# The low halves of a mixer's weights move from GpSimd to VectorE

## The chip, the cores and the metric

One NeuronCore of a Trainium2 chip runs one program. The metric is the device time of one execution in microseconds (us), taken as the median of three runs. The engines are named as the profile names them: PE is TensorE, DVE is VectorE, ACT is ScalarE, POOL is GpSimd, SP is SyncE. Each engine carries out its own instructions in the order in which the program lists them, and engines wait for one another on semaphores.

## The reference, cut to what matters

Two layers of a trunk are applied to 128 context tokens and 128 latent tokens. Each layer is a token mixer and then a channel mixer (a dense one in layer 0, eight experts in layer 1). The change touches the token mixer alone:

```python
u = h @ P['w_in'][l]                       # 1024 -> 9216: queries, keys, values, gates
...                                        # retention, neighbourhood attention, gated recurrence
proj = jnp.einsum('nbtw,nwd->btnd', br, P['w_br'][l])
gates = jax.nn.sigmoid(mg.reshape(B, T, N_BRANCH, D_MODEL))
out = jnp.sum(gates * proj, axis=2) @ P['w_o'][l]
```

So a layer's mixer has three large products: with `w_in`, with `w_br` (three branches, each then multiplied by a gate and added up) and with `w_o`.

## The kernel before, in words

**Split products.** A 32-bit product is made from three products of operands that were split into a high and a low half: `product` (line 949) issues high times low, low times high and high times high (lines 951 to 953), each 512 columns wide. So every weight block exists three times: as loaded (`ring`), its high half (`m_hi`, written by ACT in `mix_split`, line 700), and its low half (`ring_lo`, loaded value minus high half, a subtraction of 128x2048 elements by DVE at line 1630 or by POOL at line 551).

**Slabs and units.** The mixer of a layer reads 23 slabs in a fixed order: panels 0 to 13 of `w_in`, branch 0 of `w_br`, panels 14 and 15, branch 1, panels 16 and 17, branch 2, and two halves of `w_o`. Each slab is two units of 2048 columns, numbered m = 0 to 45; unit m belongs to slab m // 2. A panel of `w_in` is slab c = j up to panel 13; panel 14 is slab 15, panel 15 is slab 16, panel 16 is slab 18, panel 17 is slab 19. There are three buffers for high halves, so ACT may make the high half of unit m only when PE has finished unit m - 3 (`mix_used`).

**The order on each engine** is written out by hand:

- PE runs panel j, then small products of the branches (`pieces`), and after panels 13, 15 and 17 the projection of a branch (`project`), followed for the first two by one step of the recurrence (`level`, line 1013). `panel(l, j)` for j of 14 or more begins with a wait on `pr_read`: the first half of branch 0's projection must have been read from its PSUM bank before panel 14 can write there, the second half before panel 15, and the same for branch 1 with panels 16 and 17.
- ACT makes the high half of one unit before it reads a finished panel and of one after it; at a branch it makes two more.
- DVE calls `ahead(l, kind, i)` once for each slab c. It makes the low halves of units 2c + 3 and 2c + 4. Between these calls stand the steps of the branches: `level_read` (line 1607) and `products` (lines 1592 to 1603, eight multiplications of 128x512) for the recurrence, `heads_turned` (line 1613), and `gated` (lines 1647 and 1650), which multiplies the projection of a branch by its gate, half by half, and by that counts up `pr_read`. Directly ahead of `gated(l, 0)` stands `ahead(l, "br", 0)` with units 31 and 32, and directly ahead of `gated(l, 1)` stands `ahead(l, "br", 1)` with units 37 and 38.
- POOL holds a list `POOL_UNITS`: the first units of slabs 12 to 19, that is m = 24, 26, 28, 30, 32, 34, 36 and 38. For these DVE's `mix_split` returns at once, and POOL makes the low half as soon as the high half is there. POOL's low halves are counted on a semaphore of their own (`mix_lo_pool`); PE's `unit` asks `mix_lo_made` which semaphore and which count to wait for.

Of the kernel before, what the change touches and what calls it, by code (L numbers as in the profile page):

```python
# [20 lines left out]
F32 = mybir.dt.float32  # L21
# [3 lines left out]
ALU = mybir.AluOpType  # L25
# [20 lines left out]
UNIT = 2048  # L46
# [38 lines left out]
MIX_SLABS = [[key for key in layer_slabs(l) if key[0] in ("win", "br", "wo")] for l in range(L)]  # L85
MIX_UNITS = 2 * len(MIX_SLABS[0])
STEP = {key[0:1] + key[2:]: c for c, key in enumerate(MIX_SLABS[0])}


POOL_UNITS = [2 * c + 4 for c in range(STEP["win", 10], STEP["win", 15] + 2)]  # L90


def ring_plan():

    uses, before, at, plan = [0] * SLOTS, [None] * SLOTS, 0, {}
    for l in range(L):
        todo = layer_slabs(l)
        if l == 0:
            todo += [("ffn", 0, i) for i in range(NFS)]
        for key in todo:  # L100
            s = at % SLOTS
            at += 1
            if key[0] != "skip":
                plan[key] = (s, uses[s], before[s])
                uses[s] += key[0] != "ffn"
                before[s] = key
    assert at % SLOTS == 0
    return plan, before


def program(nc, x, c_t, b_mod_t, norm_t, lb_t, decay, hgn, rpb, cache_kt, cache_v, s_ret, s_hg, router, consts, levels,
            w_mod, w_in, w_br, w_o, w_ff, y, new_k, new_v, new_ret, new_hg):
    plan, before0 = ring_plan()
    dense_loads = [len(range(s, NFS, SLOTS)) for s in range(SLOTS)]

    with ExitStack() as ctx:
# [3 lines left out]
        def sem(name):  # L120
            return ctx.enter_context(nc.semaphore(name))

        def shared(whole, parts):

            with ExitStack() as first:
# [4 lines left out]
        ring, ring_lo = [r[0][0] for r in rings], [r[1][0] for r in rings]  # L130
# [16 lines left out]
        m_hi = [r[:, 2 * UNIT:3 * UNIT] for r in ring_lo]  # L147
        rv_hi = rv_hi.rearrange("p (g c) -> p g c", g=2)
        rg_hg = rg_hg.rearrange("p (g c) -> p g c", g=2)
        nv = nv.rearrange("p (g c) -> p g c", g=2)  # L150
        (gate,), (pick_r, pickT_r, _) = shared([("gate", 2 * D)], [("pick", 2 * 2 * P), ("pickT", 2 * 2 * P), ("gate_rest", D)])
        gates = gate.rearrange("p (g c) -> p g c", g=2)
        q_dec = gate[:, 0:2 * W].rearrange("p (d h t) -> p d h t", d=2, h=H)
        decays = gate[:, 2 * W:3 * W].rearrange("p (h t) -> p h t", h=H)
        bias = gate[:, 3 * W:4 * W].rearrange("p (h t) -> p h t", h=H)
        (u,), (_, act_hi, act_lo, hr_hi, hr_lo, eo_hi, eo_lo) = shared(
            [("u", 11 * D)], [("u_head", 2 * D), ("act_hi", W), ("act_lo", W), ("hr_hi", 2 * D), ("hr_lo", 2 * D),
                              ("eo_hi", 2 * D), ("eo_lo", 2 * D)])
# [76 lines left out]
        def con_(name):  # L235
            return con[:, CONST_AT[name]:CONST_AT[name] + CONST_W[name]]
# [83 lines left out]
        brt_read = sem("brt_read")  # L320
        mix_hi = sem("mix_hi_ready")
        mix_lo = sem("mix_lo_ready")
        mix_lo_pool = sem("mix_lo_pool_ready")
        mix_half = sem("mix_half_used")
        mt_hi = sem("merged_hi_ready")
        lev_ready = sem("lev_ready")
# [64 lines left out]
        def mix_unit(l, m):  # L391

            return MIX_SLABS[l][m // 2], m % 2, (MIX_UNITS * l + m) % SLOTS, MIX_UNITS * l + m

        def mix_lo_made(l, m):

            if m in POOL_UNITS:
                return mix_lo_pool, len(POOL_UNITS) * l + POOL_UNITS.index(m) + 1
            return mix_lo, (MIX_UNITS - len(POOL_UNITS)) * l + m + 1 - sum(v < m for v in POOL_UNITS)

        def mix_used(l, m):

            key, half, _, count = mix_unit(l, m)
            return released(key) if half else (mix_half, count // 2 + 1)
# [93 lines left out]
        @block.gpsimd  # L498
        def _(pool):
            pool.dma_start(cond, c_t).then_inc(s_cond, 16)  # L500
            for dst, src in ((con, consts), (bm, b_mod_t), (ng, norm_t), (lbr, lb_t), (dec, decay),
                             (rout_w, router), (level_mask, levels)):
                pool.dma_start(dst, src).then_inc(s_const, 16)
            pool.dma_start(x_sb, x).then_inc(s_x, 16)

            def power(out, in_, done, n):
                pool.tensor_tensor(out, in_, con_("half")[:, 0:1].broadcast_to([P, n]), ALU.pow).then_inc(done, 1)

            for l in range(L):
                if l:  # L510

                    pool.wait_ge(pr_read, 6 * l)
                pool.dma_start(bias, rpb[l]).then_inc(s_bias, 16)
                if l:

                    pool.wait_ge(pv_done, l)
                    pool.wait_ge(ho_done, l)
                pool.dma_start(ckT, cache_kt[l]).then_inc(s_cache, 16)
                pool.dma_start(cv, cache_v[l]).then_inc(s_cache, 16)
                pool.dma_start(state0, s_ret[l]).then_inc(s_sret, 16)  # L520
                if l:
                    pool.wait_ge(br_ready, 3 * l)
                pool.dma_start(hgn_sb, hgn[l]).then_inc(s_hgn, 16)
                if l == 0:
                    pool.wait_ge(s_const, 16 * 7)
                pool.wait_ge(ms_ready, 4 * l + 1)
                power(rs, ms, rs_ready, 2)

                pool.wait_ge(kd_ready, 1)
                pool.wait_ge(win_read, NWIN * l + 2)  # L530
                for d in range(2):
                    for h in range(H):
                        last = pool.tensor_scalar(kdec[:, d, h * HD:(h + 1) * HD], stage[:, 1, 0, h * HD:(h + 1) * HD],
                                                  kd[:, l, d, h:h + 1], None, ALU.mult)
                last.then_inc(kdec_ready, 1)
                pool.wait_ge(ve_ready, l + 1)
                power(hrs, hms, rsr_ready, 8)
                pool.wait_ge(win_read, NWIN * l + 6)
                pool.dma_start(new_k[l], stage[:, 1, 0, :]).then_inc(s_kout, 16)
                pool.wait_ge(win_read, NWIN * l + 7)  # L540
                pool.dma_start(new_v[l], nv[:, 0, :]).then_inc(s_vout, 16)
                pool.wait_ge(rst_read, l + 1)
                pool.dma_start(new_ret[l], state_out).then_inc(s_srout, 16)
                pool.wait_ge(ro_done, l + 1)
                pool.dma_start(state0, s_hg[l]).then_inc(s_shg, 16)
                for m in POOL_UNITS:
                    key, half, b, count = mix_unit(l, m)
                    s = plan[key][0]
                    part = slice(half * UNIT, (half + 1) * UNIT)
                    pool.wait_ge(mix_hi, count + 1)  # L550
                    pool.tensor_tensor(ring_lo[s][:, part], ring[s][:, part], m_hi[b].bitcast(F32), ALU.subtract)\
                        .then_inc(mix_lo_pool, 1)
                pool.wait_ge(hms_ready, l + 1)
                power(hrs, hms, hrs_ready, 8)
                pool.wait_ge(hst_read, l + 1)
                pool.dma_start(new_hg[l], state_out).then_inc(s_shout, 16)
                for n in (1, 2, 3):
                    pool.wait_ge(ms_ready, 4 * l + n + 1)
                    power(rs, ms, rs_ready, 2)
            pool.wait_ge(x_new, 2 * L)  # L560
            pool.dma_start(y, x_sb).then_inc(s_yout, 16)
# [350 lines left out]
        def _(pe):  # L912
# [42 lines left out]
            def unit(l, step, half, blocks):  # L955

                pe.wait_ge(*mix_lo_made(l, 2 * step + half))
                key, half, b, count = mix_unit(l, 2 * step + half)
                pe.wait_ge(mix_hi, count + 1)
                lo = ring_lo[plan[key][0]][:, half * UNIT:(half + 1) * UNIT]  # L960
                return [v.rearrange("p (k c) -> p k c", k=blocks) for v in (m_hi[b], lo)]
# [443 lines left out]
        def _(dve):  # L1405
# [215 lines left out]

            def mix_split(l, m):

                if m in POOL_UNITS:
                    return
                key, half, b, count = mix_unit(l, m)
                s = plan[key][0]
                dve.wait_ge(mix_hi, count + 1)
                part = slice(half * UNIT, (half + 1) * UNIT)
                V.tensor_tensor(ring_lo[s][:, part], ring[s][:, part], m_hi[b].bitcast(F32), ALU.subtract).then_inc(mix_lo, 1)  # L1630

            def ahead(l, kind, i):

                for m in (2 * STEP[kind, i] + 3, 2 * STEP[kind, i] + 4):
                    mix_split(l, m)
# [184 lines left out]
            for l in range(L):  # L1820
# [3 lines left out]
                if l:  # L1824
                    mix_split(l, 0)
# [9 lines left out]
                if l == 0:  # L1835
                    mix_split(0, 0)
                    own(read_mod(1), mod_read, 1)
                    modulation(0, 2, 6, mod_raw[:, 8 * MOD_FIRST:2 * NMOD], mod_rest, 1)
# [191 lines left out]
```

## Time and profile before

| | |
|---|---|
| median of three runs (lowest, highest) | 1937.44 us (1936.02, 1938.24) |
| time of the profiled execution | 1936.62 us |
| its span in the profile | 1934.8 us |
| mean granted clock of PE | 0.963 of full speed |
| busy: PE, DVE, ACT, POOL | 93%, 65%, 51%, 7% of the span |

The span is what the profiler sees from the first to the last instruction; the execution's own time is 1.8 us longer. Stages in time: modulation until about 170 us, mixer of layer 0 from there to about 499 us, the dense channel mixer until about 740 us, mixer of layer 1 to about 1067 us, and the experts until the end. The units in question are used between about 320 and 440 us and between about 888 and 1007 us. In the timeline each line gives the start, the duration, engine, line and operation, and in brackets the idle time before it on its engine and what ended it. In layer 1 the same instructions stand 567 us later with nearly the same durations, so most rows below are of layer 0.

### The profile page before, as it was taken

Reading aid. Unit: us, or ns where it says so; the run is one execution under the profiler, and the core shown is the slowest. Engines: PE = TensorE matmul, PEld = TensorE weight load, DVE = VectorE, ACT = ScalarE, POOL = GpSimd, SP = SyncE. Lnnn points to the kernel's source line nnn. Section 1 sums busy time; section 2 is a strip of 40 time slices with the busy share of each in tenths; the row PEclk is TensorE's granted clock in tenths of the full one; section 3 lists DMA queues with packets and bytes.
Section 4 is the critical chain, followed back from the end, with each engine's and each line's share of the span. In section 5 each row is a group of like instructions: output and inputs, shape, how many; then the busy total and the mean of one; then the engine's idle time right before and its main releaser. Section 6 shows DMA issues by size and latency. Waiting matters only on the chain.

```text
span 1934.8 us, 20304 instructions
## 1 busy us (share of the span) xinstructions
PE 1809.0 (93%) x8206; PEld 1414.5 (73%) x8206; DVE 1250.1 (65%) x1053; ACT 988.6 (51%) x966; POOL 126.4 (7%) x78
## 2 busy tenths in 40 slices
PE   8999999997699986999998599999999999999995
PEld 1224888886578865888876578888888888888884
DVE  1102567984354525658884378888888888888883
ACT  2101435333444326345332367777777777777772
POOL 1000201320000000102320000000000000000000
PEclk9999999998899997999998699999999999999998
DMA  9887454341544432454332369989898999898990
GB/s 396 297 305 265 177 200 174 134 172 55 201 169 186 162 138 83 160 207 172 132 131 98 152 239 352 365 334 366 339 358 341 359 345 362 337 366 340 363 372 26
DMA packets 55822, 470.60 MB, mean 243 GB/s; under 512 B 6352, under 2 KB 6400, under 8 KB 8496
## 3 DMA queue, kind: packets, MB, share of 16 engines
q1 hardware_dynamic: 52848, 458.25, 62.2%
q0 software_dynamic: 2880, 11.02, 1.4%
q8 instruction: 68, 1.11, 0.2%
q14 instruction: 26, 0.21, 0.0%
HBM read 465.05 MB, written 4.19 MB: 243 GB/s over the span
## 4 chain that ended last, share of the span: by engine, by line
PE 91%; DVE 3%; ACT 3%; issue 2%; DMA 0%; POOL 0%; POOLq 0%; ACTq 0%; DVEq 0%
PE ps L951 25%; PE ps L952 24%; PE ps L953 24%; PE ps L926 9%; PE ps L1127 2%; PE ps L1013 1%; PE ps L1079 1%; PE ps L1161 1%; PE ps L993 1%; PE ps L945 1%; ACT ring_lo L700 0%; DMA ring<-in_w_mod 0%; ACT wide L627 0%; PE ps L1384 0%; DVE x_sb L1685 0%
## 5 line engine op out<-in xcount | busy, mean ns | idle before, releaser
L1691 DVE TENSOR_TENSOR ring_lo<-ring,w_hi 128x2048 fp32r<-128x2048 f32 x297 | 680.1, 2292 | 178.9 <-ACT w_hi L711 178.2
L951 PE MATMUL ps<-ring_lo,h_both 128*128 128x512 f32 x1520 | 609.0, 401 | 23.7 <-issue 16.3
L711 ACT ACTIVATE w_hi<-ring 128x2048 fp32r<-128x2048 f32 x297 | 567.9, 1915 | 102.7 <-PE ps L953 93.6
L1630 DVE TENSOR_TENSOR ring_lo<-ring,ring_lo 128x2048 fp32r<-128x2048 f32 x76 | 182.6, 2405 | 265.6 <-ACT ring_lo L700 265.0
L951 PEld LDWEIGHTS ps<-ring_lo,h_both 128*128 128x128 f32 x1520 | 288.2, 190 | 82.6 <-issue 24.3
L952 PE MATMUL ps<-w_hi,h_both 128*128 128x512 f32 x880 | 345.6, 393 | 0.0
L953 PE MATMUL ps<-w_hi,h_both 128*128 128x512 f32 x880 | 345.6, 393 | 0.0
L700 ACT ACTIVATE ring_lo<-ring 128x2048 fp32r<-128x2048 f32 x92 | 176.2, 1917 | 323.3 <-PE ps L953 210.7
L952 PE MATMUL ps<-ring_lo,h_both 128*128 128x512 f32 x640 | 251.5, 393 | 0.0
L953 PE MATMUL ps<-ring_lo,h_both 128*128 128x512 f32 x640 | 251.4, 393 | 0.0
L953 PEld LDWEIGHTS ps<-w_hi,h_both 128*128 128x128 f32 x880 | 166.6, 189 | 35.5
L952 PEld LDWEIGHTS ps<-w_hi,h_both 128*128 128x128 f32 x880 | 167.1, 190 | 32.2
L951 PE MATMUL ps<-ring_lo,act_hi 128*128 128x512 f32 x440 | 177.6, 404 | 9.4 <-DVE ring_lo L1691 9.4
L926 PE MATMUL ps<-ring,cond_pad 128*36 128x512 f32 (+1 forms) x384 | 167.7, 599 | 9.4 <-DMA ring<-in_w_mod 9.4
L953 PE MATMUL ps<-w_hi,act_hi 128*128 128x512 f32 x440 | 173.6, 395 | 0.0
L952 PE MATMUL ps<-w_hi,act_lo 128*128 128x512 f32 x440 | 173.4, 394 | 0.0
L953 PEld LDWEIGHTS ps<-ring_lo,h_both 128*128 128x128 f32 x640 | 121.6, 190 | 25.9
L952 PEld LDWEIGHTS ps<-ring_lo,h_both 128*128 128x128 f32 x640 | 121.8, 190 | 24.2
L926 PEld LDWEIGHTS ps<-ring,cond_pad 128*36 128x36 f32 (+1 forms) x384 | 41.6, 109 | 133.7 <-issue 133.7
L951 PEld LDWEIGHTS ps<-ring_lo,act_hi 128*128 128x128 f32 x440 | 83.9, 191 | 25.1 <-DVE ring_lo L1691 9.9
L953 PEld LDWEIGHTS ps<-w_hi,act_hi 128*128 128x128 f32 x440 | 83.6, 190 | 17.8
L952 PEld LDWEIGHTS ps<-w_hi,act_lo 128*128 128x128 f32 x440 | 83.9, 191 | 15.1
(269 smaller groups left out, 1524.8 us busy)
## 6 DMA issues: line engine op xcount, KB each, us to landing
ring<-in_w_ff SPq DMA_DIRECT2D x297, 1024.0 KB, 7.2
ring<-in_w_in SPq DMA_DIRECT2D x36, 2048.0 KB, 7.8
ring<-in_w_mod SPq DMA_DIRECT2D x24, 2048.0 KB, 7.8
ring<-in_w_br SPq DMA_DIRECT2D x6, 2048.0 KB, 7.8
ring<-in_w_o SPq DMA_DIRECT2D x4, 2048.0 KB, 7.7
out<-state_out POOLq DMA_DIRECT2D x4, 512.0 KB, 4.5
x_sb<-in_x POOLq DMA_DIRECT2D x1, 1024.0 KB, 23.7
state<-in_s_ret POOLq DMA_DIRECT2D x2, 512.0 KB, 20.8
```

Source lines behind the costliest of these rows:

```text
L700: A(m_hi[b], ring[s][:, half * UNIT:(half + 1) * UNIT], ACT.Copy).then_inc(mix_hi, 1)
L711: A(w_hi[p], ring[slab_slot(n)][:, p * UNIT:(p + 1) * UNIT], ACT.Copy).then_inc(hi_ready[p], 1)
L926: ins = mm(ps[0:height, part, :], cond_pad[:, k, at:at + height], w[:, k, :], start=(i == 0 and k == 0), stop=(n == slabs[-1] and k == KD ...
L945: ins = nc.tensor.transpose(ps[:, 4 + 2 * g + k // 4, (k % 4) * P:(k % 4 + 1) * P], xn[:, g, k * P:(k + 1) * P], ident)
L951: mm(out, a_hi, b_lo, start=start, stop=False, skip_group_check=True)
L952: mm(out, a_lo, b_hi, start=False, stop=False, skip_group_check=True)
L953: return mm(out, a_hi, b_hi, start=False, stop=stop, skip_group_check=True)
L993: ins = nc.tensor.transpose(ps[:, 6 + g, h * P:(h + 1) * P], src[:, h * HD:(h + 1) * HD], ident)
L1013: ins = mm(ps[:, 6 + u // 4, (u % 4) * P:(u % 4 + 1) * P], k_lev[:, u * P:(u + 1) * P], q[:, u * P:(u + 1) * P], start=True, stop=True)
L1127: ins = mm(out[:, v * P:(v + 1) * P], rows[:, g, k * P:(k + 1) * P], pick[:, b, g, :], start=(g == 0), stop=(g == 1))
L1630: V.tensor_tensor(ring_lo[s][:, part], ring[s][:, part], m_hi[b].bitcast(F32), ALU.subtract).then_inc(mix_lo, 1)
L1691: V.tensor_tensor(ring_lo[slot][:, part], ring[slot][:, part], w_hi[p].bitcast(F32), ALU.subtract)\
```

## The change

The list `POOL_UNITS`, its semaphore and POOL's loop are removed. DVE's `mix_split` no longer skips those units, so `ahead` now makes both of its units on DVE, in program order. PE waits on one semaphore, counted in unit order.

```diff
-POOL_UNITS = [2 * c + 4 for c in range(STEP["win", 10], STEP["win", 15] + 2)]
...
-        mix_lo_pool = sem("mix_lo_pool_ready")
...
         def mix_lo_made(l, m):
 
-            if m in POOL_UNITS:
-                return mix_lo_pool, len(POOL_UNITS) * l + POOL_UNITS.index(m) + 1
-            return mix_lo, (MIX_UNITS - len(POOL_UNITS)) * l + m + 1 - sum(v < m for v in POOL_UNITS)
+            return mix_lo, MIX_UNITS * l + m + 1
...
                 pool.wait_ge(ro_done, l + 1)
                 pool.dma_start(state0, s_hg[l]).then_inc(s_shg, 16)
-                for m in POOL_UNITS:
-                    key, half, b, count = mix_unit(l, m)
-                    s = plan[key][0]
-                    part = slice(half * UNIT, (half + 1) * UNIT)
-                    pool.wait_ge(mix_hi, count + 1)
-                    pool.tensor_tensor(ring_lo[s][:, part], ring[s][:, part], m_hi[b].bitcast(F32), ALU.subtract)\
-                        .then_inc(mix_lo_pool, 1)
                 pool.wait_ge(hms_ready, l + 1)
                 power(hrs, hms, hrs_ready, 8)
...
             def mix_split(l, m):
 
-                if m in POOL_UNITS:
-                    return
                 key, half, b, count = mix_unit(l, m)
                 s = plan[key][0]
                 dve.wait_ge(mix_hi, count + 1)
```

## Rows read from the trace of the kernel before

**Rows 1.** The page: busy time of engines, and the chain's shares by engine.
```profile
PE 1809.0 (93%) x8206; PEld 1414.5 (73%) x8206; DVE 1250.1 (65%) x1053; ACT 988.6 (51%) x966; POOL 126.4 (7%) x78
...
PE 91%; DVE 3%; ACT 3%; issue 2%; DMA 0%; POOL 0%; POOLq 0%; ACTq 0%; DVEq 0%
```

**Rows 2.** Timeline of PE: start, duration, instruction, idle time before it.
```profile
371.15 1.95 PE L1013 MATMUL ps<-u 128*128 128x128 f32 x16
374.72 0.47 PE L951 MATMUL ps<-ring_lo,h_both 128*128 128x512 f32 x1 [1.63 <-issue]
...
415.50 0.47 PE L951 MATMUL ps<-ring_lo,h_both 128*128 128x512 f32 x1 [1.59 <-issue]
...
470.64 2.48 PE L1040 MATMUL ps<-con,wide 128*128 128x128 f32 x16 [3.87 <-DVE wide L1650]
...
942.19 0.47 PE L951 MATMUL ps<-ring_lo,h_both 128*128 128x512 f32 x1 [1.63 <-issue]
...
1038.17 3.36 PE L1040 MATMUL ps<-con,wide 128*128 128x128 f32 x16 [3.87 <-DVE wide L1650]
```

**Rows 3.** Timeline of DVE, layer 0, around products and gates.
```profile
342.71 0.70 DVE L1592 TENSOR_TENSOR u<-u 128x512 f32<-128x512 f32 x1
...
347.79 2.29 DVE L1630 TENSOR_TENSOR ring_lo<-ring,ring_lo 128x2048 fp32r<-128x2048 f32 x1
...
371.19 2.29 DVE L1630 TENSOR_TENSOR ring_lo<-ring,ring_lo 128x2048 fp32r<-128x2048 f32 x1
373.40 2.48 DVE L1647 TENSOR_TENSOR wide<-ps,gate 128x1024 f32<-128x1024 f32 x2
375.91 1.38 DVE L1607 COPY_PREDICATED u<-level_mask,ps 128x1024 f32<-128x1024 int32 x1
...
411.97 2.29 DVE L1630 TENSOR_TENSOR ring_lo<-ring,ring_lo 128x2048 fp32r<-128x2048 f32 x1
414.18 1.22 DVE L1647 TENSOR_TENSOR br<-ps,gate 128x1024 f32<-128x1024 f32 x1
```

**Rows 4.** Timeline of ACT, layer 0: high halves of units 28, 30, 32, 36, 38.
```profile
346.08 1.92 ACT L700 ACTIVATE ring_lo<-ring 128x2048 fp32r<-128x2048 f32 x1
...
359.64 1.92 ACT L700 ACTIVATE ring_lo<-ring 128x2048 fp32r<-128x2048 f32 x1
...
371.40 1.92 ACT L700 ACTIVATE ring_lo<-ring 128x2048 fp32r<-128x2048 f32 x1 [3.52 <-PE ps L953]
...
400.45 1.92 ACT L700 ACTIVATE ring_lo<-ring 128x2048 fp32r<-128x2048 f32 x1
...
412.22 1.91 ACT L700 ACTIVATE ring_lo<-ring 128x2048 fp32r<-128x2048 f32 x1 [3.24 <-PE ps L953]
```

**Rows 5.** Groups of POOL's instructions: count, busy us and mean ns, idle before.
```profile
L551 POOL TENSOR_TENSOR ring_lo<-ring,ring_lo 128x2048 fp32r<-128x2048 f32 x16 | 77.5, 4841 | 218.2 <-ACT ring_lo L700 218.2
```

**Rows 6.** Groups of DVE's instructions between 300 and 437 us.
```profile
L1630 DVE TENSOR_TENSOR ring_lo<-ring,ring_lo 128x2048 fp32r<-128x2048 f32 x13 | 34.2, 2627 | 7.6 <-ACT ring_lo L700 7.3
L1592 DVE TENSOR_TENSOR u<-u 128x512 f32<-128x512 f32 x7 | 16.3, 2335 | 0.0
...
L1571 DVE TENSOR_SCALAR u<-u,olb,lb 128x256 f32<-128x256 f32 x8 | 6.2, 842 | 2.3 <-ACT u L863 2.3
L1650 DVE TENSOR_TENSOR wide<-wide,br 128x1024 f32<-128x1024 f32 x2 | 5.7, 2832 | 0.1
...
L1593 DVE TENSOR_TENSOR u<-u 128x512 f32<-128x512 f32 x7 | 4.8, 684 | 0.0
```

**Rows 7.** Stretches: length, busy PE, PEld, DVE, ACT, POOL, granted clock, DMA.
```profile
374.70:378.70 4.00, 3.98 (x18) 3.29 (x19) 3.96 (x4) 0.00 (x0) 3.31 (x1) 1.00 0.79 340
...
475.40:478.80 3.40, 3.26 (x8) 2.62 (x9) 2.33 (x2) 1.05 (x1) 0.00 (x0) 0.51 0.00 0
...
1038.50:1041.90 3.40, 3.03 (x15) 2.63 (x13) 0.98 (x1) 1.36 (x2) 0.00 (x0) 0.51 0.95 407
...
710.20:714.30 4.10, 4.10 (x10) 3.23 (x11) 0.00 (x0) 0.00 (x0) 0.00 (x0) 0.50 0.35 146
```

## The prediction

> **What bounds the kernel now.** I first read the busy times on the page and the chain of waits: PE is busy 93% of the span and makes 91% of the chain, POOL is busy 7% [rows 1]. So an edit on DVE or POOL moves the time only where PE ends up waiting for it. I then looked for PE's idle stretches in the stage that the change touches. The timeline of PE shows just two per layer worth naming, in the same places: before panel 14, 1.63 us ahead of 374.72, and before panel 16, 1.59 us ahead of 415.50; layer 1 repeats the first at 942.19 and the second likewise, so four in all [rows 2]. The releaser is given as "issue", which tells nothing, so I looked at what the program waits for there: panel 14 needs the first half of `gated(l, 0)`. On DVE's timeline two of line 1647 start at 373.40 and take 2.48 us; the first ends at about 374.62, and PE starts 0.1 us later. The other place fits as well: 414.18 plus 1.22 is 415.40, and PE starts at 415.50 [rows 2, 3]. So DVE's arrival at `gated` sets these two starts, and what DVE has to do just ahead of it is what counts.
>
> **What the change removes.** On POOL, 16 subtractions of 4.84 us in the mean, 77.5 us [rows 5]. POOL is not on the chain, and its next step after the list waits for sums that are made much later, so this alone is worth 0.
>
> It also removes a disturbance of DVE. Lines 1592 and 1593 do the same amount of work, but seven of 1592 take 16.3 us and seven of 1593 4.8: 11.5 too much. In the same stretch 13 of line 1630 average 2.63 instead of 2.29 us (4.4 too much), two of line 1650 take 5.7 where two multiplications of that size take 2.48 (3.2), and eight of line 1571 take 6.2 where half of line 1593 each would be 2.7 (3.5) [rows 3, 6]. Together 22.6 us per layer, and I take all of it to go with POOL's work. Bounds: 0 if the delays have another cause, 22.6 if not; I take 22.6, because it falls on a few instructions of several kinds while their neighbours keep their length, as eight blockings per layer would make it.
> The Trainium skill says it in "SBUF — State Buffer", section "Who interferes with whom": GpSimd and VectorE share one port pair that is held for a whole instruction, and the other engine stops entirely; the rows bear this out. By that rule alone, removing GpSimd's work should make VectorE's queue shorter; the sum that this gives is the fourth rival below.
>
> **What it adds on DVE.** Eight subtractions per layer. One lasts 2.29 us, and the next instruction starts 2.21 us after it (371.19 to 373.40) [rows 3]: 17.7 us per layer. That is less than the 22.6 us given back, so DVE gets no busier. What matters is where they stand: in program order, each behind a wait for ACT's high half, with everything after it on DVE queued behind.
>
> **The place before panel 14.** ACT starts the high half of unit 32 at 371.40, when PE has finished unit 29, and ends at 373.32 [rows 4]. Now DVE first makes unit 32's low half and only then comes to `gated`. Is DVE there in time? I replay from unit 30, whose high half ends at 359.64 + 1.92 = 361.56 [rows 4]. Subtraction 2.21, `level_read` 1.38 (line 1607), `products` 5.08 undisturbed (342.71 to 347.79), subtraction of unit 31 2.21 [rows 3]: 372.4. DVE is thus free 0.9 us before unit 32's high half is there. (It is at unit 30 in time too: from unit 28, ready at 348.0, two subtractions, `heads_turned` (1.22, as line 1647, which has the same size), `level_read` and `products` end at 360.1 [rows 3, 4].) So: high half 373.32, subtraction from 373.35 to 375.56, first half of `gated` to 376.78, PE at 376.88 in place of 374.72: **2.16 us later**, a stall of 3.8 us in place of 1.63. Neither the time given back nor an earlier start helps, since ACT cannot make this high half before PE's projection ends.
>
> **The place before panel 16.** All times shift with PE, so I reckon on the old clock. Unit 36's high half ends at 402.37; subtraction, `level_read`, `products` and the subtraction of unit 37 end at 413.3; unit 38's high half ends at 412.22 + 1.91 = 414.13 [rows 3, 4]. Subtraction to 416.37, gate to 417.59, PE at 417.69 in place of 415.50: **2.19 us**, a stall of 3.8 in place of 1.59. Both places in both layers: 2 x (2.16 + 2.19) = 8.7 us.
>
> The other six units cost nothing: PE uses each about a slab after its high half is made (three slabs and what lies between take from 374.72 to 415.50, 13.6 us each [rows 2]), and DVE returns to waiting for ACT in between, as the two replays show. Past panel 16 nothing on DVE is new, and the rest shifts as a whole.
>
> **The clock.** A longer stall may cost more than its length. After the 1.6 us stalls the granted clock stays at 1.00 (2.4 GHz), as in 374.70 to 378.70 [rows 7]. But the trace has two stalls of 3.87 us, ahead of 470.64 and of 1038.17 [rows 2], and PE's clock fell right behind both: 0.51 in 1038.50 to 1041.90 and 0.51 in 475.40 to 478.80 (1.2 GHz) [rows 7]. Directly: 16 transposes took 3.36 us behind the stall at 1038.17, and 16 matmuls of that size 1.95 at 371.15 [rows 2]. My stalls of 3.8 us are almost as long, so I expect the same four times. Half of PE's busy time in such a stretch is lost: 3.03 / 2 = 1.5, 3.26 / 2 = 1.6, and after a stall of nearly 5 us 4.10 / 2 = 2.05 [rows 7]. Bounds 0 and 2.05 each; I take 1.6, by the two stalls of my length: 4 x 1.6 = 6.4 us.
>
> **Sum.** 1936.62 (the profiled execution's own time, span 1934.8) + 8.7 + 6.4 = 1951.7. The median of runs lies 0.8 above that execution, which would make 1952.5; I forecast 1952.
>
> **Rivals.**
> 1. *The clock holds.* The two 3.87 us stalls stand among other idle stretches; mine stand between full panels. Then only 8.7 us are lost: 1945.3, on the median 1946.1. For it: the 1.6 us stalls leave the clock alone. Against it: of the two stalls of that length neither left the clock alone.
> 2. *The delays on DVE do not go.* If POOL is not their cause, five extra subtractions (11 us) lie ahead of panel 14, less the half of DVE's 9.9 us of waits in the stretch [rows 6]: 6 us; before panel 16 at least 2.2. With 2 us of clock each: 2 x (6 + 2.2 + 4) = 24, so 1961. For it: that POOL delays DVE is inferred from two lists, not shown instruction by instruction. Against it: no other work in the stretch comes eight times and then stops.
> 3. *No change.* PE's start at panels 14 and 16 might hang on something else that ends with `gated` by chance, and that is 2.2 us later anyway: 1937. Against it: two places with the same 0.1 us between, and the wait in the program.
> 4. *Faster.* If PE were held by DVE's queue as a whole in this stage, the time given back would decide: 2 x (22.6 - 17.7) = 9.8 us, 1927. It decides if units 32 and 38 are subtracted before `gated` is due, that is if their high halves end 2.2 us earlier than the rows show. Against it: PE waits at only two places per layer, and at both it is ACT's high half, on PE's own clock, that DVE then waits for.
>
> **Chances.** Forecast 0.66; rival 1 0.20; rival 2 0.05; rival 3 0.04; rival 4 0.05. The range takes in rival 1 and, at the upper end, all four clock falls at 2.05 (1953.5) with 2 us for DVE's 0.9 us margins being smaller than I reckon: 1944 to 1956; rivals 2, 3 and 4 lie outside with 0.14. No change means within 0.2%, about 4 us, which is what a measurement of this kernel can tell. Forecast, rival 1 and rival 2 are slower: 0.91; rival 3 0.04; rival 4 0.05.
>
> **What would show it.** In the changed kernel's profile POOL's busy time falls to about 49 us and its group of subtractions is gone; the group of line 1592 averages near 0.69 us; DVE's subtraction of unit 32 starts right behind ACT's high half and `gated` right behind it; PE's idle time before panels 14 and 16 is 3.8 us in both layers, with the granted clock at 0.5 for some 3 us behind each. It is wrong if those stalls stay at 1.6 us, if the clock stays at 1.0 behind them, or if a third place in the stage makes PE wait.

## The result, and the profile after

The changed kernel takes 1952.17 us (median of 4 runs, 1951.71 to 1954.41) beside 1937.84 us for the kernel before: a ratio of 1.0077, 95% interval 1.006 to 1.0095. It is slower, by 14.3 us: little, but the interval leaves out 1. The profiled execution took 1951.71 us, its span is 1949.7. Line numbers of the instructions below are 13 to 15 lower than in the kernel before.

The page: busy time of engines, and the chain by engine (it answers to [rows 1]).

```profile
PE 1815.4 (93%) x8206; PEld 1419.7 (73%) x8206; DVE 1240.4 (64%) x1069; ACT 987.9 (51%) x966; POOL 48.6 (2%) x62
...
PE 91%; DVE 3%; ACT 3%; issue 2%; DMA 0%; POOL 0%; POOLq 0%; ACTq 0%; DVEq 0%
```

DVE has 16 instructions more and is busy 9.7 us less: what it took over costs less than the blocking that went away. POOL lost its 78 us. Both engines became less busy, and the kernel became slower.

The timeline of PE after (it answers to [rows 2]): the four starts that the prediction named.

```profile
369.96 1.95 PE L1000 MATMUL ps<-u 128*128 128x128 f32 x16
...
375.69 0.76 PE L938 MATMUL ps<-ring_lo,h_both 128*128 128x512 f32 x1 [3.79 <-issue]
...
421.34 0.47 PE L938 MATMUL ps<-ring_lo,h_both 128*128 128x512 f32 x1 [3.79 <-issue]
...
954.36 0.47 PE L938 MATMUL ps<-ring_lo,h_both 128*128 128x512 f32 x1 [3.79 <-issue]
...
998.93 0.47 PE L938 MATMUL ps<-ring_lo,h_both 128*128 128x512 f32 x1 [3.79 <-issue]
```

Each idle time in brackets is 3.79 us where it was 1.63 or 1.59. The timelines of DVE and of ACT after, ahead of the first of them (they answer to [rows 3, 4]), say why:

```profile
368.91 2.29 DVE L1615 TENSOR_TENSOR ring_lo<-ring,ring_lo 128x2048 fp32r<-128x2048 f32 x1
372.17 2.29 DVE L1615 TENSOR_TENSOR ring_lo<-ring,ring_lo 128x2048 fp32r<-128x2048 f32 x1 [0.96 <-ACT ring_lo L687]
374.38 2.48 DVE L1632 TENSOR_TENSOR wide<-ps,gate 128x1024 f32<-128x1024 f32 x2
```

```profile
370.22 1.91 ACT L687 ACTIVATE ring_lo<-ring 128x2048 fp32r<-128x2048 f32 x1 [3.52 <-PE ps L940]
```

Unit 31 is subtracted first. Then DVE sits idle 0.96 us for ACT's high half of unit 32, which ends at 372.13, and subtracts unit 32. Only then come the gates, the first of which lets PE start at 375.69.

Groups of DVE's instructions between 300 and 445 us after (count, busy us and mean ns, idle before; they answer to [rows 6]):

```profile
L1615 DVE TENSOR_TENSOR ring_lo<-ring,ring_lo 128x2048 fp32r<-128x2048 f32 x21 | 48.1, 2292 | 29.7 <-ACT ring_lo L687 29.4
...
L1580 DVE TENSOR_TENSOR u<-u 128x512 f32<-128x512 f32 x7 | 4.9, 696 | 0.0
...
L1579 DVE TENSOR_TENSOR u<-u 128x512 f32<-128x512 f32 x7 | 4.8, 689 | 0.0
...
L1558 DVE TENSOR_SCALAR u<-u,olb,lb 128x256 f32<-128x256 f32 x8 | 2.8, 410 | 0.4 <-ACT u L850 0.4
L1635 DVE TENSOR_TENSOR wide<-wide,br 128x1024 f32<-128x1024 f32 x2 | 2.4, 1224 | 0.1
```

Line 1579 (1592 before) now takes as long as its neighbour 1580, and all the other excess is gone too.

Stretches of the two profiles show where the time went (length, busy PE, PEld, DVE, ACT, POOL, granted clock, DMA). Their bounds are the same points of the program: the end of branch 0's projection, the end of panel 17, the transposes at the start of layer 1, again the first two in layer 1, and the end. Before:

```profile
0.00:371.15 371.15, 360.29 (x1365) 204.96 (x1365) 145.89 (x176) 108.82 (x127) 42.70 (x36) 1.00 0.67 248
371.15:439.18 68.03, 64.81 (x329) 54.96 (x328) 58.65 (x49) 23.01 (x17) 18.42 (x4) 1.00 0.43 155
439.18:737.12 297.94, 247.60 (x1142) 205.41 (x1140) 130.40 (x98) 112.87 (x116) 7.76 (x11) 0.92 0.40 152
737.12:938.61 201.49, 196.51 (x972) 166.33 (x973) 139.06 (x154) 97.66 (x111) 34.15 (x17) 0.96 0.43 154
938.61:1006.61 68.00, 64.78 (x329) 54.96 (x328) 58.64 (x49) 23.02 (x17) 18.40 (x4) 1.00 0.43 155
1006.61:1934.80 928.19, 875.05 (x4075) 727.85 (x4073) 717.42 (x530) 623.26 (x578) 4.94 (x6) 0.96 0.78 303
```

After:

```profile
0.00:369.96 369.96, 359.29 (x1364) 204.96 (x1365) 142.74 (x181) 108.81 (x127) 22.26 (x32) 1.00 0.67 249
369.96:446.62 76.66, 69.09 (x330) 58.06 (x328) 57.08 (x52) 22.99 (x17) 0.00 (x0) 0.93 0.38 137
446.62:748.70 302.08, 251.76 (x1142) 208.58 (x1140) 130.38 (x98) 112.77 (x116) 7.69 (x11) 0.90 0.39 150
748.70:948.63 199.93, 194.95 (x972) 165.40 (x973) 135.82 (x159) 97.48 (x111) 13.75 (x13) 0.97 0.43 155
948.63:1024.18 75.55, 67.98 (x329) 57.24 (x328) 57.08 (x52) 22.99 (x17) 0.00 (x0) 0.95 0.39 140
1024.18:1949.70 925.52, 872.30 (x4075) 725.48 (x4073) 717.28 (x530) 622.83 (x578) 4.91 (x6) 0.96 0.78 304
```

The stretch that holds both stalls grew by 8.63 us in layer 0 and by 7.55 in layer 1, 16.2 together, and its granted clock fell from 1.00 to 0.93 and 0.95. The other stretches together are 1.3 us shorter (one is 4.1 longer, the others 1.2 to 2.7 shorter). PE's work in them is unchanged, although some of the moved subtractions lie in the first and the fourth.

### The profile page after: what moved, and what is told of

It reads as the page before. It is cut to its first block, busy times and chain, and to the rows that moved or that the text cites. A ratio compares the mean times of both kernels' runs of the same rounds, so it can differ in the third digit from the quotient of the medians.

```text
span 1949.7 us, 20304 instructions
## 1 busy us (share of the span) xinstructions
PE 1815.4 (93%) x8206; PEld 1419.7 (73%) x8206; DVE 1240.4 (64%) x1069; ACT 987.9 (51%) x966; POOL 48.6 (2%) x62
## 4 chain that ended last, share of the span: by engine, by line
PE 91%; DVE 3%; ACT 3%; issue 2%; DMA 0%; POOL 0%; POOLq 0%; ACTq 0%; DVEq 0%
PE ps L938 25%; PE ps L940 24%; PE ps L939 24%; PE ps L913 9%; PE ps L1114 1%; PE ps L1000 1%; PE ps L1066 1%; PE ps L1148 1%; PE ps L932 1%; PE ps L980 1%; ACT ring_lo L687 0%; ACT wide L614 0%; DMA ring<-in_w_mod 0%; DVE x_sb L1670 0%; DVE ring_lo L1676 0%
## 5 line engine op out<-in xcount | busy, mean ns | idle before, releaser
L1615 DVE TENSOR_TENSOR ring_lo<-ring,ring_lo 128x2048 fp32r<-128x2048 f32 x92 | 210.4, 2290 | 310.2 <-ACT ring_lo L687 309.7
L938 PEld LDWEIGHTS ps<-ring_lo,h_both 128*128 128x128 f32 x1520 | 290.5, 191 | 91.8 <-issue 33.3
L940 PEld LDWEIGHTS ps<-ring_lo,h_both 128*128 128x128 f32 x640 | 123.2, 192 | 26.5
L939 PEld LDWEIGHTS ps<-ring_lo,h_both 128*128 128x128 f32 x640 | 123.5, 193 | 25.0
```

The source lines that it names most:

```text
L938: mm(out, a_hi, b_lo, start=start, stop=False, skip_group_check=True)
L939: mm(out, a_lo, b_hi, start=False, stop=False, skip_group_check=True)
L940: return mm(out, a_hi, b_hi, start=False, stop=stop, skip_group_check=True)
```

## The experiments

Theory A is the prediction's: the loss comes from units 32 and 38, which stand between ACT's high half and a gate, and has two terms, the longer stall and the clock behind it. Rival B is that DVE's queue as a whole counts. Rival C is that only the length of the stalls counts. Rival D is that POOL's blocking of DVE costs nothing. "Stretch" below is the one from the end of branch 0's projection to the end of panel 17.

The first two experiments and the last are edits of the kernel before and keep its line numbers; the others are edits of the changed kernel. Ratios and differences are to the kernel before as it ran beside each: a median of 1936.59 us, and 1935.85 beside "only the second unit behind the gate" and the last experiment.

**POOL keeps units 32 and 38 only**

```diff
-POOL_UNITS = [2 * c + 4 for c in range(STEP["win", 10], STEP["win", 15] + 2)]
+POOL_UNITS = [2 * STEP["br", i] + 4 for i in (0, 1)]
```

> POOL makes units 32 and 38 only, DVE the other six, in program order. Theory A (the cost lies in the two units that stand ahead of the gates, 2.2 us of longer stall each, and the clock behind it): the stalls before panels 14 and 16 vanish as far as DVE's subtraction made them; DVE comes to the gate 1.07 us earlier than in the kernel before, because POOL no longer holds it up before, so the stalls are 0.5 us in place of 1.6 and the time is 1937.8 - 4 x 1.07 = 1933.5 us. Rival B (DVE's queue as a whole counts, each of the eight units alike): six of eight units of the loss stay, 1937.8 + 14.3 x 6/8 = 1948.5 us.

Measured: 1929.4 us, ratio to the kernel before 0.996 (0.9947 to 0.9973). PE's idle time before the four panels is 0.51 to 0.53 us. The two stretches:

```profile
370.54:436.39 65.85, 64.81 (x329) 54.96 (x328) 58.51 (x50) 23.00 (x17) 9.23 (x2) 1.00 0.44 160
...
936.07:1001.94 65.87, 64.82 (x330) 54.96 (x328) 58.52 (x50) 23.00 (x17) 9.22 (x2) 1.00 0.44 160
```

They are 2.18 and 2.13 us shorter than before, 4.3 together, as theory A had it; six of eight units moved to DVE cost nothing, so rival B falls. The time fell by 7.2 us, 3 more than the stretches explain: the rest lies outside of them (see the end of this section).

**DVE takes units 32 and 38 only**

```diff
-POOL_UNITS = [2 * c + 4 for c in range(STEP["win", 10], STEP["win", 15] + 2)]
+POOL_UNITS = [2 * c + 4 for c in range(STEP["win", 10], STEP["win", 15] + 2) if c not in (STEP["br", 0], STEP["br", 1])]
```

> The opposite: DVE makes units 32 and 38 only, POOL the other six. Theory A: the whole loss is there, stalls of 3.8 us or a little more (POOL's work still delays DVE), the clock falls behind them, 1952 us. Rival B: two of eight units, 1937.8 + 14.3 x 2/8 = 1941.4 us.

Measured: 1953.69 us, ratio 1.0084 (1.0071 to 1.0097): the whole loss with a quarter of the edit. PE's stalls:

```profile
376.18 0.77 PE L951 MATMUL ps<-ring_lo,h_both 128*128 128x512 f32 x1 [3.82 <-issue]
...
421.88 0.47 PE L951 MATMUL ps<-ring_lo,h_both 128*128 128x512 f32 x1 [3.79 <-issue]
```

**The same work on DVE, both units behind the gates**

```diff
-                ahead(l, "br", 0)
                 gated(l, 0)
+                mix_split(l, 2 * STEP["br", 0] + 3)
+                mix_split(l, 2 * STEP["br", 0] + 4)
...
-                ahead(l, "br", 1)
                 gated(l, 1)
+                mix_split(l, 2 * STEP["br", 1] + 3)
+                mix_split(l, 2 * STEP["br", 1] + 4)
```

> The changed kernel (no low halves on POOL), but DVE makes units 31 and 32 just behind the first gate and 37 and 38 just behind the second, instead of ahead of them. DVE does the same work in the stage. Theory A: the gate is done before PE's step of the recurrence ends, the four stalls are 0 in place of 1.6 in the kernel before, 1937.8 - 6.4 = 1931.4 us. Rival B: the same work on DVE, about 1952 us.

Measured: 1925.7 us, ratio 0.9943 (0.993 to 0.9956). Both stretches take 64.28 us, and PE is busy through all of it:

```profile
370.66:434.94 64.28, 64.28 (x330) 54.81 (x329) 56.78 (x52) 23.00 (x17) 0.00 (x0) 1.00 0.45 164
```

On DVE the gates now follow `products` directly, and the two subtractions stand behind them:

```profile
368.88 0.68 DVE L1590 TENSOR_TENSOR u<-u 128x512 f32<-128x512 f32 x1
369.60 2.55 DVE L1632 TENSOR_TENSOR wide<-ps,gate 128x1024 f32<-128x1024 f32 x2
372.18 4.49 DVE L1615 TENSOR_TENSOR ring_lo<-ring,ring_lo 128x2048 fp32r<-128x2048 f32 x2
```

This kernel does the changed kernel's work on every engine and beats both kernels, 0.57% below the kernel before. What the change cost is a matter of order alone.

**Only the second unit behind the gate**

```diff
-                ahead(l, "br", 0)
+                mix_split(l, 2 * STEP["br", 0] + 3)
                 gated(l, 0)
+                mix_split(l, 2 * STEP["br", 0] + 4)
...
-                ahead(l, "br", 1)
+                mix_split(l, 2 * STEP["br", 1] + 3)
                 gated(l, 1)
+                mix_split(l, 2 * STEP["br", 1] + 4)
```

> The changed kernel, with only units 32 and 38 behind the gates; 31 and 37 stay ahead. Theory A: DVE comes to the gate when unit 31 is done, as in the kernel with units 32 and 38 on POOL: stalls of 0.5 us, each layer's stretch from the end of branch 0's projection to the end of panel 17 65.9 us (68.0 in the kernel before, 76.7 and 75.6 in the changed one), and the time as there, 1929 to 1932 us. Rival B (DVE's queue as a whole): 1952 us.

Measured: 1929.34 us, ratio 0.9965 (0.9954 to 0.9976), with stalls of 0.51 to 0.53 us: the same as with units 32 and 38 on POOL.

**Matmuls in the stall**

```diff
                         if j < NWIN - 1:
                             level(l, 3 if j == 13 else 6)
+                            for _ in range(12):
+                                mm(ps[:, 4, :], h_hi[:, 0, 0, :], h_hi[:, 0, 0:4, :], start=True, stop=True)
```

> The changed kernel, with 12 matmuls of 512 columns (2.7 us at full clock) added on PE at each of the four stalls; nobody reads their result. They lie inside the 3.8 us stall, so the panel begins at the same moment, but PE is not idle. Theory A with the clock as its second term: the clock stays at 1.0 and the 6.4 to 7.3 us lost at half clock come back, 1945 to 1946 us. Rival C (only the length of the stalls counts): 1952 us, or more by the added work.

Measured: 1942.12 us, ratio 1.0024 (1.0014 to 1.0034), some 10 us below the changed kernel although PE does more. The stretch, and PE's first stall:

```profile
370.81:443.17 72.36, 70.26 (x353) 59.16 (x352) 57.06 (x52) 23.00 (x17) 0.00 (x0) 1.00 0.40 146
```

```profile
376.54 0.47 PE L938 MATMUL ps<-ring_lo,h_both 128*128 128x512 f32 x1 [1.05 <-issue]
```

The stretches are 72.36 and 72.38 us, 4.33 and 4.38 above the kernel before, at a granted clock of 1.00. That is 8.7 us, the first term of the sum by itself. Panel 14 begins 5.73 us after the start of the stretch here and in the changed kernel alike, so what the changed kernel's stretches have above these (4.30 and 3.17 us) comes after the stall and is the clock's. Rival C falls.

**POOL's eight units, with the gates first**

```diff
-                ahead(l, "br", 0)
                 gated(l, 0)
+                ahead(l, "br", 0)
...
-                ahead(l, "br", 1)
                 gated(l, 1)
+                ahead(l, "br", 1)
```

(on the kernel before)

> The kernel before (POOL makes its eight units), with units 31 and 37 moved behind the gates. Theory A with POOL blocking DVE: the 1.6 us stalls before panels 14 and 16 go, but POOL starts unit 32 just before DVE gets to unit 31, DVE is held up until POOL is done, and panels 14 and 16 wait in their middle for units 31 and 37: some 1.7 us in the first, some 3 us in the second, so 1937 to 1943 us, no better than before. Rival D (POOL's presence costs nothing, only the order on DVE counts): no stalls, 1936.6 - 6.4 = 1930 us, like the kernel with units 31, 32, 37 and 38 on DVE behind the gates.

Measured: 1939.28 us, ratio 1.0018 (1.0009 to 1.0027). The better order gains nothing while POOL works; the time is 3.4 us longer. POOL, then DVE, at the first gate:

```profile
372.16 4.60 POOL L551 TENSOR_TENSOR ring_lo<-ring,ring_lo 128x2048 fp32r<-128x2048 f32 x1 [7.16 <-ACT ring_lo L700]
```

```profile
369.93 2.48 DVE L1647 TENSOR_TENSOR wide<-ps,gate 128x1024 f32<-128x1024 f32 x2
372.44 6.47 DVE L1630 TENSOR_TENSOR ring_lo<-ring,ring_lo 128x2048 fp32r<-128x2048 f32 x1
```

DVE's subtraction starts 0.28 us behind POOL's, and lasts POOL's remaining 4.3 us plus its own 2.2. It is unit 31, the second half of panel 14, and likewise unit 37 is that of panel 16, so PE waits for them in the middle of these panels:

```profile
378.97 0.50 PE L951 MATMUL ps<-ring_lo,h_both 128*128 128x512 f32 x1 [1.65 <-DVE ring_lo L1630]
...
421.24 0.50 PE L951 MATMUL ps<-ring_lo,h_both 128*128 128x512 f32 x1 [3.02 <-DVE ring_lo L1630]
```

1.65 and 3.02 us (1.67 and 3.03 in layer 1), where some 1.7 and 3 were expected; rival D falls. The two stretches are 3.2 and 4.4 us longer than before, and the clock is part of it:

```profile
369.92:441.13 71.21, 66.54 (x329) 55.80 (x328) 61.87 (x48) 22.98 (x17) 18.53 (x4) 0.98 0.41 148
...
941.35:1013.77 72.42, 67.73 (x330) 56.72 (x328) 61.88 (x48) 22.98 (x17) 18.55 (x4) 0.95 0.40 145
```

Without POOL's units, putting the gates first takes the ratio to the kernel before from 1.0077 to 0.9943; with them, from 1 to 1.0018.

**What stays open.** The time does not follow the stretches alone. Five of the six experiments' kernels are 2.2 to 4.2 us faster than their two stretches explain (the changed kernel 1.9), which is why three of them came out below the time expected; the kernel with two units on DVE is 0.9 slower. By their profiles this lies in stages where PE's work is the same and the granted clock differs. From the start of layer 1 to the end of its first projection, for example, the kernel before shows 201.49 us at 0.96 and the changed kernel 199.93 at 0.97, with the same idle time of PE, 4.98 us. The same stall can go either way: in layer 0, some 7 us after panel 17, PE waits 2.3 us for ACT, and behind that wait the clock is 1.00 in the kernel before (the first row) and 0.50 in the one with only the second unit behind the gate (the second):

```profile
446.09:449.40 3.31, 2.05 (x16) 1.86 (x16) 1.82 (x8) 1.02 (x1) 1.45 (x1) 1.00 0.00 0
```

```profile
442.29:445.40 3.11, 3.11 (x14) 3.11 (x15) 1.63 (x7) 0.00 (x0) 1.45 (x1) 0.50 0.00 0
```

Runs of the kernel before itself spread over 7 us (1934.05 to 1940.83 in 14 runs), and of each kernel there is one profile. That the clock's low stretches fall otherwise was read from the profiles and not tested, and why most of these kernels gain by it is not known.

## Why the prediction was right

- **The bound and the places.** PE waited at the two places per layer that were named, at no third in that stage, and by the wait that was named. Moving two units behind the gate took the waits away.
- **The stall.** Forecast 3.8 us in place of 1.6, four times, 8.7 us. Measured 3.79 four times; with the clock held up, 8.7 us.
- **DVE in time.** The replay had DVE 0.9 us early at unit 32; it sat idle 0.96 us there, and 0.96 before unit 38.
- **The blocking.** 22.6 us per layer were taken to go; the groups show every excess gone. The bound of 0 (rival "the delays on DVE do not go") fell. The last experiment shows instruction by instruction what the prediction inferred from two lists: DVE stops until POOL has finished. The Trainium skill ("SBUF — State Buffer", "Who interferes with whom") describes it so, and 6.47 us against 2.29 agrees.
- **The clock.** Forecast 1.6 us per stall, 6.4; the stretches give 4.3 and 3.2 us per layer, 7.5. The mechanism was right and the size too small. In the first stall the clock fell before PE started again (0.86 over the stall, the first row below), and PE then worked at half clock for the 5.5 us of the second row: a loss of some 2.75 us, above the bound of 2.05. Behind the others it fell some 1 us after the restart or sooner and stayed low for some 3.4 us. These are stretches of the changed kernel, the first stall and what stands behind the first two:

```profile
371.90:375.69 3.79, 0.01 (x1) 0.03 (x1) 3.49 (x3) 0.23 (x1) 0.00 (x0) 0.86 0.87 363
375.69:381.19 5.50, 5.50 (x13) 4.33 (x14) 5.47 (x8) 0.00 (x0) 0.00 (x0) 0.50 0.20 83
...
421.34:422.30 0.96, 0.96 (x4) 0.83 (x5) 0.96 (x1) 0.00 (x0) 0.00 (x0) 1.00 1.00 427
422.30:425.80 3.50, 3.50 (x10) 2.69 (x10) 3.40 (x4) 0.00 (x0) 0.00 (x0) 0.52 0.06 19
```

  The profile before could have shown this. Of the two stalls that sized the term, the prediction read the one at 470.64 by the stretch 475.40 to 478.80 [rows 7], which is only the second half of the low clock behind it. The whole of it is:

```profile
471.94:478.76 6.82, 4.40 (x15) 3.35 (x13) 4.73 (x3) 3.79 (x3) 0.00 (x0) 0.50 0.20 86
```

  Half of 4.40 is 2.2 us where 1.6 was taken (with a second wait of 2.42 us inside). With 2.2 and 1.5 for the two stalls the estimate for four would have been 7.4.

- **The sum.** 8.7 + 7.5 is 16.2; the rest of the execution was 1.3 us shorter, so 14.9 on the span. The forecast of 1952 was met in part because a clock term 1.1 too small and a rest that shrank by 1.3 offset each other.
- **The rivals.** "The clock holds" fell by the granted clock; the kernel with matmuls in the stall is what it would have looked like. "Faster" named the right thing, the time that DVE gets back, and the right condition, that units 32 and 38 must not stand ahead of the gate; but an earlier high half is not the only way to meet it. Moving the subtraction behind the gate does it too. "No change" fell with the waits, which go when the gate moves ahead.

## What to carry to other kernels

When work moves to another engine, its length matters less than what stands behind it in that engine's program: here a queue that got shorter in total became later at the one instruction that PE waits for. Put what releases the bottleneck ahead of work that is needed later (here half a slab or a whole one), above all if that work has to wait for something itself. Then look for what else can hold that work up: with POOL's blocking, half a slab was too little. And reckon a stall of TensorE with what its clock loses behind it, here nearly as much again (7.5 us) as the stalls' growth (8.7).

## What the runs showed of the hardware that was not expected

- A stall of 3.02 us inside a panel, with full work on both sides, was enough to bring the clock down: in the last experiment PE's matmuls behind 421.24 are first 0.24 and then 0.43 us apart. Stalls of 1.6 us left it alone in all four places of the kernel before, and the 1.65 us in the middle of panel 14 did so too. Between short matmuls 2.3 us was enough in one kernel and not in another (the two rows under "what stays open").

```profile
421.58 0.40 PE L952 MATMUL ps<-ring_lo,h_both 128*128 128x512 f32 x1
421.82 0.56 PE L953 MATMUL ps<-ring_lo,h_both 128*128 128x512 f32 x1
422.18 0.63 PE L951 MATMUL ps<-ring_lo,h_both 128*128 128x512 f32 x1
422.61 0.63 PE L952 MATMUL ps<-ring_lo,h_both 128*128 128x512 f32 x1
```

- DVE's multiplication that reads PSUM and one operand of SBUF was not held up by POOL: two of line 1647 took their usual 2.48 us while POOL was at work [rows 3]. Line 1650, with both operands in SBUF, took 4.44 us beside POOL where it takes 1.22. These are the timelines of POOL and of DVE in the kernel before:

```profile
373.40 4.61 POOL L551 TENSOR_TENSOR ring_lo<-ring,ring_lo 128x2048 fp32r<-128x2048 f32 x1 [7.13 <-ACT ring_lo L700]
...
414.21 4.58 POOL L551 TENSOR_TENSOR ring_lo<-ring,ring_lo 128x2048 fp32r<-128x2048 f32 x1 [7.16 <-ACT ring_lo L700]
```

```profile
415.43 4.44 DVE L1650 TENSOR_TENSOR wide<-wide,br 128x1024 f32<-128x1024 f32 x1
```
